# Mixture-of-experts stage on one NeuronCore: experts of two blocks, of one block and pairs of small ones in a repeated pattern of six in five steps

## The reference, cut to what matters

```python
score = sigmoid(h @ w_router)                          # 576 tokens, 64 experts
idx   = top_k(score + router_bias, 8)
g     = 2.5 * score[idx] / sum(score[idx])
for each expert e, for its tokens t:
    a       = silu(h[t] @ w_gate_e[e]) * (h[t] @ w_up_e[e])     # 1024 -> 256
    acc[t] += (a @ w_down_e[e]) * g[t, e]                       # 256 -> 1024
y = x + acc + (silu(h @ w_gate_s) * (h @ w_up_s)) @ w_down_s    # shared expert
```

## Time and profile before

| | |
|---|---|
| median of 3 runs | 1511.62 us (1509.58 to 1522.3) |
| profiled execution | 1511.85 us, its span 1510.1 us |
| TensorE matmul busy | 1364.6 us, 90% of the span |
| VectorE, ScalarE, GpSimd busy | 41%, 23%, 16% |
| chain that ended last | DMA 26% of the span, 25% the down weights; TensorE 20% |
| bytes moved by DMA | 424.10 MB, mean 281 GB/s |
| weight loads of experts | 64 each of gate, up, down |

### The profile page before, as it was taken

The page is one execution under the profiler, slowest core; times in us unless marked ns, Lnnn a source line. Parts: engine busy times, 40 slices in busy tenths (PEclk is TensorE's granted clock), DMA queues, the critical chain, the costliest instruction groups (busy, mean ns, idle before and its releaser), DMA issues. The chain is left out here.

```text
span 1510.1 us, 30180 instructions
## 1 busy us (share of the span) xinstructions
PE 1364.6 (90%) x9894; PEld 724.0 (48%) x9895; DVE 614.1 (41%) x1812; ACT 346.4 (23%) x939; POOL 246.1 (16%) x291
## 2 busy tenths in 40 slices
PE   6999889999999999899889877779999999989982
PEld 2445556666667776445543322224444443333320
DVE  1524156777575665445723222222333333332323
ACT  1202135344434443411001111111111111111110
POOL 2000110005173320000001111111222222221210
PEclk9999889999999999999989988889999999999996
DMA  7412299999989999860189999999776989999966
GB/s 310 72 28 50 67 329 298 335 371 312 330 294 311 352 331 344 296 239 31 53 343 355 369 378 374 373 373 377 239 229 209 316 307 333 383 365 358 367 224 207
DMA packets 160683, 424.10 MB, mean 281 GB/s; under 512 B 48225, under 2 KB 51842, under 8 KB 134402
## 3 DMA queue, kind: packets, MB, share of 16 engines
q1 hardware_dynamic: 142928, 381.30, 69.3%
q0 software_dynamic: 14400, 38.82, 10.6%
q10 hardware_dynamic: 3250, 2.65, 0.5%
HBM read 395.25 MB, written 41.06 MB: 289 GB/s over the span
## 5 line engine op out<-in xcount | busy, mean ns | idle before, releaser
L2584 PE MATMUL ps_gu<-ring,mixT 128*32 128x512 f32 (+2 forms) x1664 | 365.9, 634 | 52.8 <-SPq L2402 51.9
L2584 PEld LDWEIGHTS ps_gu<-ring,mixT 128*32 128x32 f32 (+2 forms) x1664 | 125.2, 141 | 289.1 <-issue 248.6
L2603 PE MATMUL ps_y<-w_dn,aT_e 128*32 128x512 f32 (+2 forms) x832 | 175.9, 598 | 4.3 <-DVE aT_e L2517 2.4
L1509 PE MATMUL ps_kT<-ident,ring 128*128 128x128 f32 x1024 | 142.3, 281 | 11.1 <-DVE ring L1132 6.2
L1509 PEld LDWEIGHTS ps_kT<-ident,ring 128*128 128x128 f32 x1024 | 115.1, 145 | 69.0 <-ACT ring L967 34.3
L2515 DVE TENSOR_TENSOR act_in<-sil,ps_gu 128x256 f32<-128x256 f32 x48 | 20.2, 421 | 284.3 <-ACT sil L2460 284.3
L1791 POOL DMA_INDIRECT kT<-h_dram,idx x50 | 51.9, 1037 | 493.9 <-DVE idx L1825 493.9
L1132 DVE COPY ring<-ps_kT 128x512 f32<-128x512 f32 x128 | 88.2, 689 | 82.1 <-PE ps_kT L1509 79.6
L2460 ACT ACTIVATE sil<-ps_gu 128x256 f32<-128x256 f32 x48 | 18.4, 384 | 400.3 <-PE ps_gu L2584 400.3
L2426 POOL DMA_INDIRECT sums_dram<-qT,sidx x48 | 76.5, 1595 | 151.2 <-DVE qT L2525 144.0
L2603 PEld LDWEIGHTS ps_y<-w_dn,aT_e 128*32 128x32 f32 (+2 forms) x832 | 55.5, 132 | 94.4 <-issue 87.2
(11 more groups left out here) (528 smaller groups left out, 1682.9 us busy)
## 6 DMA issues: line engine op xcount, KB each, us to landing
ring<-in_cache_k SPq DMA_DIRECT2D x256, 256.0 KB, 4.4
ring<-in_cache_v SPq DMA_DIRECT2D x256, 256.0 KB, 4.7
ring<-in_w_gate_e SPq DMA_DIRECT2D x64, 1024.0 KB, 9.9
ring<-in_w_up_e SPq DMA_DIRECT2D x64, 1024.0 KB, 12.7
w_dn<-in_w_down_e SPq DMA_DIRECT2D x64, 1024.0 KB, 9.7
w_in<-in_w_in SPq DMA_DIRECT2D x8, 1028.0 KB, 19.7
sums_dram<-w_dn SPq DMA_DIRECT2D x1, 4608.0 KB, 21.1
ring<-in_w_out SPq DMA_DIRECT2D x2, 2048.0 KB, 12.4
```

Of the source, the lines that this page charges most:

```text
L1509: last = pe.transpose(ps_kT[:, j % 2, e * PAGE:(e + 1) * PAGE], k_places[n % RING][:, e * DA + j * P:e * DA + (j + 1) * P], m.ident[:, :])
L2584: last = pe.matmul(ps_gu[at, :].rearrange("p (g n) -> p g n", g=2), xgT[:, u, k, at], w_gu[:, place, :, k, :].rearrange("p s g n -> p (s g ...
L2603: last = pe.matmul(ps_y[at, n, :], aT[:, j, at], w_dn[:, place, j, n * 512:(n + 1) * 512].rearrange("p s n -> p (s n)"), start=(j == 0), s ...
```

## The change

The plan forms groups of six experts in five steps: one expert of two blocks (two steps), a pair of small ones (one step), an expert of one block (one step), another pair (one step). The number K of groups is the least of (N2 - 12)/4, the experts of two blocks and those of one block in the full-width class, rounded down to even. These groups run behind the first N2 - 4K small experts; then the other full-width experts, then the four-in-three class. The loop holds two groups (ten steps; the places in the ring repeat after two groups), runs at least once, and its places are written into the code (`MIXED`). Every expert has the same number of lanes and steps as before.

The plan gets more instructions. On TensorE, `find` for steps 0 and 1 and the wait for `tables_done` lie at other points among the shared expert's matmuls. `loop_tab` has a fourth bound. SyncE's, GpSimd's, ScalarE's and VectorE's loops over the steps are unchanged.

```diff
--- before.py
+++ after.py
@@ -1761,7 +1761,7 @@
 QUAD = P // BLK
 PAIRED, TRIPLE = 4, 8
 MIN_TWO = 3 * PAIRED
-MAX_BLK = QUAD * (T * TOPK // P + NE) + 2 * MIN_TWO + 3 * TRIPLE + 2 * QUAD
+MAX_BLK = QUAD * (T * TOPK // P + NE) + 2 * MIN_TWO + 3 * TRIPLE + 2 * QUAD + 40
 TAB = 4 * P
 MAX_LOOPS = -(-MAX_BLK // (2 * QUAD))
 N_COL = 7
...
...
@@ -2109,9 +2109,11 @@
                 dve.drain()
                 dve.tensor_copy(m.pick[:, :, :, 6], part[:, :, :])
                 (count, n_big, in2, r2, of2, in3, r3, of3, of4, r4, b4, end, order, first, tmp, tmp2) = (cnt[:, i, :] for i in range(16))
+                in_d, r_d, in_s, r_s, rest4 = (biased[:, i, :] for i in range(TT))
+                of_y, of2_y, half, quarter, at_y = (rest[:, i, :] for i in range(TT))
                 stt = dve.scalar_tensor_tensor
                 ts = dve.tensor_scalar
-                N2, N3, W2, W3, B3, B4, O3, O4, ENDS = (n_f[:, i:i + 1] for i in range(9))
+                N2, N3, W3, BF, B3, K, NT, BY, O3, O4, OY, ENDS = (n_f[:, i:i + 1] for i in range(12))
                 run = lambda out, x: dve.tensor_tensor_scan(out, m.ones[:, 0:NE], x, 0.0, ALU.mult, ALU.add)
                 dve.wait_ge(rank_mm, 1)
                 dve.tensor_copy(count, ps[:, 3, TT * NE:(TT + 1) * NE])
@@ -2130,11 +2132,9 @@
                 dve.tensor_copy(N2, n_i[:, 1:2])
                 dve.drain()
                 stt(of2, r2, N2, in2, ALU.is_le, ALU.mult)
-                ts(W2, N2, float(MIN_TWO), None, ALU.max)
+                ts(K, N2, 1.0 / 4, -MIN_TWO / 4.0, ALU.mult, ALU.add)
                 dve.drain()
                 stt(in3, count, float(3 * BLK), of2, ALU.is_le, ALU.subtract)
-                ts(B4, W2, 2.0, None, ALU.mult)
-                ts(O4, N2, -1.0, None, ALU.add)
                 dve.drain()
                 run(r3, in3)
                 dve.drain()
@@ -2152,33 +2152,84 @@
                 dve.drain()
                 ts(of4, tmp, -1.0, 1.0, ALU.mult, ALU.add)
                 dve.drain()
-                run(r4, of4)
+                stt(in_d, n_big, 2.0, of4, ALU.is_equal, ALU.mult)
+                stt(in_s, n_big, 1.0, of4, ALU.is_equal, ALU.mult)
+                dve.drain()
+                run(r_d, in_d)
+                run(r_s, in_s)
+                dve.drain()
+                ts(K, K, r_d[:, NE - 1:NE], r_s[:, NE - 1:NE], ALU.min, ALU.min)
                 stt(b4, n_big, float(QUAD), of4, ALU.mult, ALU.mult)
                 dve.drain()
-                run(end, b4)
+                ts(n_i[:, 4:5], K, 0.0, None, ALU.max)
+                dve.drain()
+                ts(n_i[:, 5:6], n_i[:, 4:5], 2 * P - 2, None, ALU.bitwise_and)
+                dve.drain()
+                dve.tensor_copy(K, n_i[:, 5:6])
+                dve.drain()
+                stt(at_y, r_d, K, in_d, ALU.is_le, ALU.mult)
+                stt(tmp2, r_s, K, in_s, ALU.is_le, ALU.mult)
+                stt(NT, K, -4.0, N2, ALU.mult, ALU.add)
+                stt(O4, K, 2.0, N2, ALU.mult, ALU.add)
+                ts(BF, K, 2.0, 20.0, ALU.max, ALU.mult)
+                dve.drain()
+                tt(of_y, at_y, tmp2, ALU.add)
+                tt(r_d, r_d, at_y, ALU.mult)
+                tt(r_s, r_s, tmp2, ALU.mult)
+                ts(cnt_i[:, 0, :], r2, NT, -1.0, ALU.subtract, ALU.add)
+                stt(of2_y, r2, NT, of2, ALU.is_gt, ALU.mult)
+                ts(BY, NT, float(MIN_TWO), 2.0, ALU.max, ALU.mult)
+                ts(OY, NT, -6.0, None, ALU.add)
+                ts(O4, O4, -1.0, None, ALU.add)
+                dve.drain()
+                tt(rest4, of4, of_y, ALU.subtract)
+                tt(at_y, r_d, r_s, ALU.add)
+                ts(cnt_i[:, 1, :], cnt_i[:, 0, :], 1, None, ALU.arith_shift_right)
+                tt(BF, BF, BY, ALU.add)
+                dve.drain()
+                run(r4, rest4)
+                tt(in_d, b4, rest4, ALU.mult)
+                dve.tensor_copy(half, cnt_i[:, 1, :])
+                ts(cnt_i[:, 0, :], cnt_i[:, 1, :], 1, None, ALU.arith_shift_right)
+                ts(in_s, at_y, 6.0, OY, ALU.mult, ALU.add)
+                ts(r_d, at_y, 20.0, BY, ALU.mult, ALU.add)
+                dve.drain()
+                run(end, in_d)
+                dve.tensor_copy(quarter, cnt_i[:, 0, :])
+                stt(r_s, half, 1.0, of2_y, ALU.add, ALU.mult)
+                stt(first, tmp2, 3.0, in_s, ALU.mult, ALU.add)
                 stt(order, r2, -1.0, of2, ALU.add, ALU.mult)
                 stt(tmp, r3, O3, of3, ALU.add, ALU.mult)
-                stt(tmp2, r4, O4, of4, ALU.add, ALU.mult)
-                dve.drain()
+                dve.drain()
+                stt(quarter, quarter, 2.0, half, ALU.add, ALU.add)
                 ts(n_i[:, 0:1], end[:, NE - 1:NE], float(2 * QUAD - 1), None, ALU.add)
+                stt(at_y, r4, O4, rest4, ALU.add, ALU.mult)
+                tt(first, first, of_y, ALU.mult)
                 tt(order, order, tmp, ALU.add)
+                stt(tmp2, tmp2, 8.0, r_d, ALU.mult, ALU.add)
                 dve.drain()
                 ts(n_i[:, 1:2], n_i[:, 0:1], 8 * P - 2 * QUAD, None, ALU.bitwise_and)
-                stt(end, end, B4, of4, ALU.add, ALU.mult)
+                tt(order, order, r_s, ALU.add)
+                tt(at_y, at_y, first, ALU.add)
+                stt(end, end, BF, rest4, ALU.add, ALU.mult)
+                stt(tmp2, tmp2, -12.0, of_y, ALU.add, ALU.mult)
+                stt(quarter, quarter, 4.0, of2_y, ALU.mult, ALU.mult)
                 stt(r2, r2, 2.0, of2, ALU.mult, ALU.mult)
-                tt(order, order, tmp2, ALU.add)
-                dve.drain()
-                ts(B3, n_i[:, 1:2], float(2 * QUAD), B4, ALU.max, ALU.add)
-                tt(end, end, r2, ALU.add)
+                dve.drain()
+                ts(B3, n_i[:, 1:2], float(2 * QUAD), BF, ALU.max, ALU.add)
+                tt(order, order, at_y, ALU.add)
+                tt(end, end, tmp2, ALU.add)
+                tt(r2, r2, quarter, ALU.add)
                 stt(b4, of2, 2.0, b4, ALU.mult, ALU.add)
                 dve.drain()
                 ts(r3, r3, 3.0, B3, ALU.mult, ALU.add)
                 stt(ENDS, W3, 3.0, B3, ALU.mult, ALU.add)
+                tt(end, end, r2, ALU.add)
+                stt(b4, of3, 3.0, b4, ALU.mult, ALU.add)
                 dve.drain()
                 tt(r3, r3, of3, ALU.mult)
                 dve.drain()
                 tt(end, end, r3, ALU.add)
-                stt(b4, of3, 3.0, b4, ALU.mult, ALU.add)
                 dve.drain()
                 tt(first, end, b4, ALU.subtract)
                 for i in range(TAB // P):
@@ -2198,12 +2249,11 @@
                 dve.tensor_reduce(entry[:, :], found[:, :, :], AX.X, ALU.add).then_inc(cum_done, 1)
                 tt(m.pos[:, :, :], m.pos[:, :, :], mask[:, :, :], ALU.mult)
 
-                ts(loop_f[:, 0:1], W2[0:1, :], 1.0 / PAIRED, None, ALU.mult)
-                ts(loop_f[:, 1:2], B3[0:1, :], 1.0 / (2 * QUAD), None, ALU.mult)
-                ts(loop_f[:, 2:3], ENDS[0:1, :], 1.0 / (2 * QUAD), None, ALU.mult)
+                for i, stop in enumerate((BY, BF, B3, ENDS)):
+                    ts(loop_f[:, i:i + 1], stop[0:1, :], 1.0 / (2 * QUAD), None, ALU.mult)
                 dve.drain()
                 ts(m.pos[:, :, :], m.pos[:, :, :], 1.0, None, ALU.subtract)
-                dve.tensor_copy(m.loop_tab[:, 0:3], loop_f[:, 0:3])
+                dve.tensor_copy(m.loop_tab[:, 0:4], loop_f[:, 0:4])
 
                 dve.wait_ge(exp_mm, 1)
                 lanes = ps[0:1, 3, 0:TAB].rearrange("o (s j) -> o s j", j=QUAD)[:, :, QUAD - 1]
@@ -2332,13 +2382,13 @@
                 shared(0, 1, range(KD), 0)
                 shared(0, 1, range(KD), 1).then_inc(gu_mm, 1)
                 entries()
-                shared(1, 0, range(KD // 2), 0)
+                shared(1, 0, range(KD), 0)
+                shared(1, 0, range(KD), 1)
                 find(pe, m, ps[:, 7, 0:N_COL], 0)
-                shared(1, 0, range(KD // 2, KD), 0)
+                pe.wait_ge(tables_done, 1)
+                shared(1, 1, range(0, KD // 2), 0)
                 find(pe, m, ps[:, 7, 0:N_COL], 1)
-                shared(1, 0, range(KD), 1)
-                pe.wait_ge(tables_done, 1)
-                shared(1, 1, range(KD), 0)
+                shared(1, 1, range(KD // 2, KD), 0)
                 shared(1, 1, range(KD), 1).then_inc(gu_mm, 1)
 
 
@@ -2379,7 +2429,7 @@
         sum_done, y_out = sem("sum_done"), sem("y_out")
 
         def loops(eng):
-            return registers(nc, eng, m.loop_tab, 2, 1, 3, MAX_LOOPS)[0]
+            return registers(nc, eng, m.loop_tab, 3, 1, 3, MAX_LOOPS)[0]
 
         with nc.Block(no_gpsimd_drain=True) as block:
 
@@ -2543,8 +2593,8 @@
 
             @block.tensor
             def _(pe):
-                n_two, n_four = registers(nc, ENG.PE, m.loop_tab, 0, 2, 3, MAX_LOOPS)
-                n_loops = loops(ENG.PE)
```

(18 more changed lines are left out.)

## The result

The changed kernel takes 1470.17 us (median of 4 executions, 1466.62 to 1472.16), the kernel before beside it 1513.53 us. The ratio is 0.9731, with a 95% interval of 0.9698 to 0.9765: 2.7% faster, where 1468.0 in a range of 1461 to 1487 was forecast. The profiled execution has a span of 1467.3 us, against 1510.1.

A forecast was written before the change was run, and what follows sets the result against it. TensorE was taken to wait for weights in a DMA-short stage, before one leaving DMA idle. From 1511.85 us, 50.4 saved in steps 5 to 30, plus 5.0 at the start and 1.5 of DMA shortage: 1468.0, range 1461 to 1487.

The forecast's parts named there:

- Steps 5 to 30: Expert steps 5 to 30: 25 steps of 12.6 us, 315.0 in place of 365.36, 50.4 us less, the whole gain.
- DMA shortage in the mixed stage and after: Four groups lose 0.6 us each to DMA, 2.4 in all; singles behind give some back, 1.5 us kept.
- The balance itself: Mixed stage: a group of five steps and six experts needs 63.0 us of TensorE and 63.6 us of DMA.
- the weak form of the first rival: Mixed stage under the skill's 358 GB/s: a group takes 64.2 us, the sum some 2.5 us larger.
- The plan: VectorE's plan arithmetic before the first weight load: 11.4 us in place of 4.10, `entry` 7.1 us later.
- The start: Step 0 starts 5 us later, between 1.6 and 9, because TensorE waits for the plan and runs at low clock.
- lie behind TensorE: At step 0: weights 8 us later are there at 775, before 783.3, so they don't set the start.
- Mixed stage short of DMA: Rival: 8.41 us of DMA per expert, 67.4 a group; four groups cost 17.4 in place of 1.5; 1484, chance 0.20.
- Turn-around of the ring: Rival: a group's second pair gets its weights 5.4 us late, 8.2 a group, 33 in all; 1500, chance 0.07.
- Half a plan: Rival: one expert of two blocks misread, K is 2, four pair steps stay slow, 25 us back; 1493, chance 0.03.
- Blank groups: Rival: K below 2, mixed loop runs ten steps with no expert, 126 us more; 1643, chance 0.02.
- w: DMA time of one expert's 3 MB of weights where DMA is full, 7.78 us, from two full stretches.

The follow-up runs named there:

- k_two: Changed kernel with the number of groups K held at 2 in place of 4; ratio 0.9895 to the kernel before, span 1491.7 us.
- after_again: The changed kernel as it is, run once more; ratio 0.9703 to the kernel before, last sil 704.6 us from the plan's start.
- pad_before: Kernel before with 42 idle VectorE instructions in its plan and the changed kernel's TensorE order of find, shared and tables_done; ratio 1.0054 to the kernel before.
- old_places: Changed kernel with find and the wait for tables_done back at their places of the kernel before; ratio 0.9759 to the kernel before.
- after: First profiled execution of the changed kernel, nothing else altered; span 1467.3 us, ratio 0.9731 to the kernel before.
- regs_first: Changed kernel with SyncE's eight register reads ahead of its waits for the first four experts' weights; ratio 0.9689 to the kernel before.
- regs_no_wait: As regs_first, and the fifth expert's gate and up loads issued without first waiting for the fourth's landing; ratio 0.9704 to the kernel before.
- fill: On top of regs_no_wait, eight of the shared expert's matmuls moved ahead of entries(); ratio 0.9652 to the kernel before.
- fill_again: The kernel of fill run once more; ratio 0.9713 to the kernel before.
- heavy_after: Changed kernel with 256 KB more to load per expert from the fifth on; span 1526.0 us, 58.7 more.
- light_before: Kernel before with weight loads cut to 1.125 MB in place of 3 per expert from the fifth on; span 1428.3 us.

## Why the prediction was right

**Steps 5 to 30: right.** -50.4 us was forecast and -49.3 measured, with 48 steps and 64 experts as counted. That K was 4 and not 2 shows in k_two, where holding it at 2 brought 20 to 23 us back.

**DMA shortage in the mixed stage and after, 1.5 us: right in size, wrong in place.** In the mixed stage it was nothing (265.5 us for 21 steps with the full loads, 265.6 with light ones). What is above 12.6 us a step, 1.1 us in 25 steps, comes without any shortage. The 1.5 us are in the last stage (231.7 against 230.3), whose waits begin three steps sooner, at step 33, where the forecast had none over 1 us before step 36; that the last stage would begin as before was not quite so. The balance itself, 63.6 us of DMA to 63.0 of TensorE, held: share 0.99, 360 GB/s, and more load made the stage longer at once. The Trainium skill ("DMA: Bandwidth & Descriptors", section Bandwidth) puts the limit between HBM and SBUF at about 358 GB/s for a core, and says beside it that a core has about that much when both cores of a pair stream. The stage ran at 360 and lost nothing to DMA, and full stretches of before ran at 375 and 365, so here, with one core at work, it isn't the limit, and the weak form of the first rival falls.

**The plan: right.** 11.4 us in place of 4.10 were forecast for the stretch, 10.85 measured; `entry` 6.5 us later against 7.1; the first load 8.1 later against 8.

**The start: the size was right by luck, the reason wrong.** I forecast step 0 5 us later and from there on the old distances. Step 0 was 1.6 us later and step 5 4.8; in after_again, counted from the plan's start, 2.8 and 7.1. The step that failed is the sentence that the weights "lie behind TensorE". That is true of step 0, which needs the first two experts. It leaves out the fifth expert, needed in step 2, whose load stands in SyncE's program behind the landing of the fourth and behind eight register reads. Where these decide, the fifth load comes 38.0 to 38.4 us behind the first. Before, that would have been at 57.0 us from the plan's start, and step 0's gate/up matmuls, for whose end the load waits too, ended at 57.4: they hid landing and reads, with half a microsecond to spare. With the first load 8 us later the fifth comes at 64.9, 6 us behind the end of step 0's matmuls (58.9): 3.3 of waiting for the landing and 2.7 of reads. I had costed what was issued and not what SyncE waits for and does between. It isn't lost DMA time as such: DMA stopped for longer at this place before (6.4 us against 4.8). Nor does all of the delay arrive: of 7.4 us at the fifth load 4.7 reach step 5, in after_again 7.1 of 8.1, in pad_before 4.5 of 9.0. What makes the rest good, and why not each time alike, no run shows. That it came out near the 5 us forecast for TensorE is chance.
TensorE's part was too large: the low clock cost 1.4 us in `entries()`, 2.1 in most other runs, and not 3.5, and old_places shows that 4 to 5 us more at step 0 would have been free.

**Rivals.** *Mixed stage short of DMA*: no step waited, out, though near. *Turn-around of the ring*: no wait in a fifth step; out. *Half a plan*: k_two shows what it would have been, 1493.02 us, where 1493 was forecast. *Blank groups*: out, 48 steps.

## What to carry to other kernels

Where one stage waits for transfers and a later one leaves them idle, work out from two full stretches what a unit of each kind costs in transfer time, and mix the kinds until both resources need the same; here that gave 50.4 us on paper and 49.3 in the trace. Then look at what the mixing makes scarce: once transfers are busy nearly from the first load to the last, look at what lies ahead of the first load, and at what the queue that issues them waits for and does between two loads, down to its register reads. Here a first load 8 to 9 us later put step 5 5 to 7 us later, and moving the reads gained some 6 us by the trace, while dropping a wait in the same place gained nothing more. Count such effects from an event inside the program, since what lies ahead of it may vary by more than they are worth.

## What the runs showed of the hardware

- SyncE's reading of eight registers took about 2.7 us behind a wait (fifth gate load 38.1 us behind the first in after, 35.4 in regs_first). At a later turn of four experts 3.2 us lie between a down load and the next gate load, but there DMA stays busy.
- In regs_first, where no read stands between the landing of the fourth expert and the fifth load, DMA was idle there for 3.3 us all the same (786 to 791 us of its span); in regs_no_wait, whose fifth load doesn't wait for that landing, its share was 1.00 from 785 to 800 us.
- An idle time of 3.3 us of TensorE ended once at the low and once at the full clock, in one program (`entries()` 4.43 us at a granted clock of 0.50 in fill, and 2.34 at 1.00 in fill_again).
- 60 more loads of 256 KB with rows of 2 KB made the span 0.98 us longer each (heavy_after); a quarter megabyte of a load in 8 KB rows is 0.65 us by w, an estimate.
- With weights at hand, steps of two experts alone take 12.49 us (light_before, steps 5 to 13: 99.9 us for eight), steps of one 12.6, and the mixed sequence 12.64.
